# Two reorderings around the first triangular inverse: block reads behind the image reads, gate rows ahead of the crossed products

## The reference

```python
proj = h @ w_in                                   # q, k, v, z and two gates per head
qkv = silu(causal_dwconv(qkv, conv_w))            # 4 taps
q, k = l2_norm(q), l2_norm(k)                     # 8 key heads, 16 value heads of 128
g = -exp(a_log) * softplus(a + dt_bias);  beta = sigmoid(b)
g = cumsum(g);  decay = exp(g_i - g_j) below the diagonal
a = strict_lower((k_beta @ k.T) * decay)
t_inv = triangular_solve(eye + a, eye)            # inverse of a unit triangular matrix per head
u = t_inv @ v_beta;  w = t_inv @ (k_beta * exp(g))
# a scan over the chunks with a state per head, then
o = rms(o) * out_gain * silu(z);  out = o @ w_out
```

## Time and profile before

| | |
|---|---|
| time, median of 3 runs | 1376.77 us (1374.51 to 1379.86) |
| the profiled execution's own time | 1376.62 us |
| its span in the profile | 1374.7 us |
| PE busy / PEld busy | 97% / 83% of the span |
| DVE / ACT / POOL busy | 65% / 52% / 14% |
| mean granted TensorE clock | 0.991 |

### The profile page before, as it was taken

The page is one execution under the profiler, slowest core; times in us unless marked ns, Lnnn a source line. Parts: engine busy times, 40 slices in busy tenths (PEclk is TensorE's granted clock), DMA queues, the critical chain, the costliest instruction groups (busy, mean ns, idle before and its releaser), DMA issues.

```text
span 1374.7 us, 18871 instructions
## 1 busy us (share of the span) xinstructions
PE 1338.4 (97%) x7177; PEld 1134.7 (83%) x7177; DVE 894.2 (65%) x1539; ACT 710.1 (52%) x1209; POOL 190.4 (14%) x342
## 2 busy tenths in 40 slices
PE   9997989899999999999999999999999999999998
PEld 9897988778888888888888887888888877888887
DVE  7885888667555468475554699875554587755553
ACT  7764464326444346464444556654444466544441
POOL 2486888500200000000000000000000000000000
PEclk9998999999999999999999999999999999999999
DMA  9766655446665545255655455066555431566552
GB/s 267 190 157 154 150 156 148 116 131 186 186 187 189 181 140 188 87 182 185 188 185 185 151 184 170 23 214 187 182 190 187 166 123 62 165 202 184 186 191 83
DMA packets 172163, 226.46 MB, mean 165 GB/s; under 512 B 11832, under 2 KB 137594, under 8 KB 172074
## 3 DMA queue, kind: packets, MB, share of 16 engines
q1 hardware_dynamic: 166976, 213.03, 49.1%
q0 software_dynamic: 3328, 10.24, 3.7%
q10 hardware_dynamic: 1770, 1.99, 0.5%
HBM read 219.77 MB, written 5.45 MB: 164 GB/s over the span
## 4 chain that ended last, share of the span: by engine, by line
PE 76%; DVE 13%; POOL 3%; DMA 3%; issue 2%; ACT 2%; SPq 0%; ACTq 0%; DVEq 0%; POOLq 0%
PE psum L961 22%; PE psum L963 22%; PE psum L962 21%; DVE w_low L708 3%; PE psum L1194 2%; PE psum L1188 2%; POOL vectors L3285 1%; PE psum L1432 1%; PE psum L1392 1%; PE psum L1465 1%; DMA ring<-in_gdn_w_in 1%; POOL vectors L3282 1%; DVE arena L2740 1%; PE psum L952 1%; DVE work L880 1%
## 5 line engine op out<-in xcount | busy, mean ns | idle before, releaser
L708 DVE TENSOR_TENSOR w_low<-ring,w_high 128x1024 fp32r<-128x1024 f32 (+3 forms) x395 | 476.5, 1217 | 319.4 <-ACT w_high L694 319.1
L694 ACT ACTIVATE w_high<-ring 128x1024 fp32r<-128x1024 f32 (+3 forms) x395 | 410.7, 1048 | 421.0 <-PE psum L963 399.9
L961 PE MATMUL psum<-w_high,hT 128*128 128x512 f32 (+2 forms) x944 | 371.1, 393 | 0.0
L963 PE MATMUL psum<-w_high,hT 128*128 128x512 f32 (+2 forms) x944 | 366.0, 388 | 0.0
L962 PE MATMUL psum<-w_low,hT 128*128 128x512 f32 (+2 forms) x944 | 365.5, 387 | 0.0
L961 PE MATMUL psum<-w_high,parts 128*128 128x512 f32 (+1 forms) x532 | 210.3, 395 | 1.1 <-DVE parts L2748 1.1
L963 PEld LDWEIGHTS psum<-w_high,hT 128*128 128x128 f32 x944 | 177.2, 188 | 36.5
L963 PE MATMUL psum<-w_high,parts 128*128 128x512 f32 (+1 forms) x532 | 206.8, 389 | 0.0
L962 PE MATMUL psum<-w_low,parts 128*128 128x512 f32 (+1 forms) x532 | 206.7, 389 | 0.0
L962 PEld LDWEIGHTS psum<-w_low,hT 128*128 128x128 f32 x944 | 177.5, 188 | 33.8
L961 PEld LDWEIGHTS psum<-w_high,hT 128*128 128x128 f32 x944 | 177.4, 188 | 33.7
(11 more groups left out here) (306 smaller groups left out, 1402.4 us busy)
## 6 DMA issues: line engine op xcount, KB each, us to landing
ring<-in_ffn_w_gate_up SPq DMA_DIRECT2D x176, 256.0 KB, 3.2
ring<-in_w_gate_up SPq DMA_DIRECT2D x176, 256.0 KB, 3.2
ring<-in_gdn_w_in SPq DMA_DIRECT2D x48, 512.0 KB, 5.5
ring<-in_ffn_w_down SPq DMA_DIRECT2D x44, 512.0 KB, 3.2
ring<-in_w_down SPq DMA_DIRECT2D x44, 512.0 KB, 3.2
ring<-in_da_w_qkv SPq DMA_DIRECT2D x24, 512.0 KB, 3.7
ring<-in_gdn_w_out SPq DMA_DIRECT2D x16, 512.0 KB, 3.8
ring<-in_mla_w_out SPq DMA_DIRECT2D x8, 512.0 KB, 4.3
```

The costliest lines, as they stand in the source:

```text
L694: nc.scalar.activation(piece_slot(w_high, n), piece_slot(ring, n), ACT.Copy).then_inc(s.w_hi, 1)
L708: nc.vector.tensor_tensor(piece_slot(w_low, n), piece_slot(ring, n), piece_slot(w_high, n).bitcast(F32), ALU.subtract).then_inc(s.w_lo, 1)
L961: mm(out, lhs[0], rhs[0], start=start, stop=False)
L963: return mm(out, lhs[1], rhs[0], start=False, stop=stop)
```

## The change

Three lists are edited; no instruction is added, removed or changed in size.

- PE, `group_0`: `gate_rows(2)` now stands ahead of `crossed(0)` and no longer behind it.
- ACT: `gate_diff(2)` now stands between the tap of tile 19 and the split of the weight piece that follows it, so that it is ahead of the split.
- POOL: `blocks_in(1)` now stands behind `units_in()` and `images_in(0)`, and no longer ahead of them. DVE's and SP's lists are the same.

```diff
@@ PE, group_0 @@
                 turned_keys(2)
                 tile(19)
+                gate_rows(2)
                 crossed(0)
-                gate_rows(2)
                 tile(20, 0, 4)
@@ ACT @@
             z_pieces(1, 3)
-            tiles(19)
+            tap(19)
             gate_diff(2)
+            split_high(act, tile_piece[19] + SPLIT)
             gate_exp(2)
@@ POOL, loop over the groups @@
                 images_out(g)
-                if g == 0:
-                    blocks_in(1)
                 if g < GROUPS - 1:
                     units_in()
                 if g == 0:
                     images_in(0)
+                    blocks_in(1)
```

## The result

| | before | after |
|---|---|---|
| median of 20 runs each, us | 1374.96 | 1381.37 |
| lowest to highest, us | 1370.43 to 1381.31 | 1376.11 to 1388.48 |
| profiled execution: own time, span, us | 1376.62, 1374.7 | 1378.34, 1376.5 |
| its mean granted clock | 0.991 | 0.990 |

The ratio after to before is 1.0041, 95% interval 1.0027 to 1.0055: some 5.6 us slower. The forecast was no change. So neither stands for its kernel, and the experiments come back to that.

A forecast was written before the change was run, and what follows sets the result against it. PE, busy 97%, was taken as the bound. At group 1's first order, 0.5 of gain left, less 1.8 for the clock, plus 1.2 of small waits, gave -0.1: 1376.62 + 0.1 = 1376.7 us; range 1371.5 to 1381.5.

The forecast's parts named there:

- The steps at group 0: Group 0: x lands at 112, gate rows fill PE's gap, second order 8.8 us earlier, 10.3 gained at the recurrence.
- The late start: POOL, group 1: later block reads make the inversion start 3.5 us late, range 1 to 4.6, against 115.92.
- The collisions: POOL's stretch from group 1's inversion to its images: 11 slow overlaps with DVE against 8, three more costing 2.7 us.
- a slack of 6.7: Group 1: x lands at 172.1, crossed products began at 178.78, leaving 6.7 us before lateness of x matters.
- the 178.2: Slower rival, group 1: once x lands past 178.2, each further microsecond of POOL's lateness is PE's.
- The clock behind the gap: Group 1: after PE's wait of nearly 10 us, crossed products cost 3.78 instead of 2.02, losing 1.8 us.
- the small waits: PE, behind group 1's crossed products: waits of 0.68 on ACT and 0.48 on DVE vanish, giving 1.2 us back.
- From there nothing of POOL's is on the way: After group 3's keys, POOL 0.9 us late, at worst moving group 3's crossed products by 0.9, absorbed by DVE's wait.
- The 3.01 us on DVE: Group 3: PE's 3.01 us wait on DVE ahead of the first order takes up POOL's 0.9 us of lateness.
- The slower rival: POOL's lateness delays PE at group 1 and again at group 3, together about 5 us: 1381.5; chance 0.15.
- its two conditions: Slower rival: blocks landing at 120.5, 4.6 us late, and collisions costing 4.5 us, so x of group 1 lands at 181.2.
- The chance of 0.05 for slower by more than 0.5%: Whole kernel: slower than 1383.7 us, needing the slower rival and more; chance 0.05.

The follow-up runs named there:

- the second execution of before: The kernel before, nothing changed, profiled once more with one execution; measured 1375.62 us.
- the changed kernel's second profile: The kernel with all three edits, nothing further changed, profiled once more with one execution; measured 1378.14 us.
- PE held back: The full change plus 24 spare products on PE ahead of group 2's gate rows, some 6 us; 1383.11 us, ratio 1.0046.
- the rows alone: Only the PE and ACT edits against the kernel before, POOL's order as before; 1376.07 us, ratio 1.0000.
- POOL late: The kernel before plus 13 small POOL fills ahead of group 1's first copy, some 4.5 us; 1380.19 us, ratio 1.0022.
- the blocks in the inversion: The PE and ACT edits, with group 1's block reads issued at step 30 of group 0's inversion; 1373.41 us, ratio 0.9998 to before.
- the blocks by ACT: The PE and ACT edits, with group 1's two block reads issued by ACT on its own queue; 1371.80 us, ratio 0.9970 to before.
- blocks alone: Only the POOL edit against the kernel before, PE and ACT as before; 1382.29 us, ratio 1.0041.
- the kernels with the other queue: Block reads on ACT's queue with PE and ACT edits, 0.9970 to before; the same with group 3's half output product ahead of its crossed products, 0.9971.

## Why the prediction was wrong

The steps at group 0 were right. x was foreseen at 112, within 111.5 to 115.5, and by its row landed at 106.59 + 7.6 = 114.2, just as PE was ready (114.1). The reading took 7.6 us with no blocks ahead of it, so blocks ahead explain only 1.3 us of the 8.9, and the 4.9 of the next round was not to be had here. The rest was as foreseen: the gate rows in the gap, the crossed products at 113.9 and full clock (114.21, 2.05 us), the second order at 121.8 (122.43), a gain of 8.2 us there where 8.8 stood. PE came to the crossed products of group 1 at 166.17, even earlier than the 168.5 foreseen. Everything behind that came out worse.

**The late start, mis-sized.** POOL's copy was put at 119.4 and came at 120.42, at the very end of the range given: 4.5 us late for 3.5. The second read was issued at 110.53, inside the 109 to 111.5 foreseen, and took 9.8 us to land, where 119.4 leaves 8.9.

**The collisions, miscounted.** Three more were counted, 2.7 us; the stretch grew by 4.05. The price was about right. The count was read from a window of before that is shifted by PE's gain but has POOL's old length and end, 129.80 to 180.00. POOL's own lateness belongs into its end. A window to 183.8 has all 12 of the splits that lay beside POOL in the end:

```profile
129.70:183.80 54.10, 14.58 (x12) 0.97 0.58 139
```

Twelve against 7 is five more, and of the masking at 119.74 only the end still meets POOL's copy (0.61 us for 0.21). Five at 0.9, less the 0.5 of the masking, are 4.0. The Trainium skill ("SBUF — State Buffer", "Who interferes with whom") has a DVE operation with two inputs in SBUF contend with a GpSimd operation that reads SBUF, under an exclusive lock. The trace agrees: only POOL operations beside such DVE operations were long, as told above, and one that began at 169.99, 0.3 us into a split from 169.68 to 171.00, ended at 171.27. The 4.05 us for five, some 0.8 each, are less than the 1.22 of a split, as it would be if POOL comes some way into most of them.

Together x was issued 8.55 us late, not 6.2, against a slack of 6.7: it landed at 180.45 and not 178.3, past the 178.2 that the prediction names as the point from which each further microsecond is PE's. This is the step that put PE behind. Of the slack itself only 1.9 us are there in the second execution of before.

**The clock behind the gap, nearly right.** The crossed products cost 3.78, as foreseen. The gate rows behind them, priced at their old 2.02, took 2.80. How far the slow clock reaches varies: they took 2.43 in the changed kernel's second profile, behind the same gap, and 1.95 with PE held back, behind 12.34 us. The first order of group 1 was so 2.7 us late against the first execution, where the prediction's sum had it 0.1 us late: 1.7 for x, 1.8 and 0.8 for the clock, less 1.2 for the small waits and 0.4 of overlapped ends.

**"From there nothing of POOL's is on the way" failed too.** The prediction had POOL reach the keys of group 3 at 194.0 and DVE's matrices ready at 193.2. POOL came at 194.5, but the matrices were late: the writing started at 196.28 instead of 193.06. They hang on PE. In the eight profiles in which POOL waits there for DVE, the writing starts 7.6 to 8.4 us behind PE's first order of group 1, so PE's 2.7 us of lateness went by way of DVE back to POOL. X of group 3 was then issued 3.8 us late by the first profile of before, and 6.1 by the second (258.61 against 252.53). PE waited 2.54 us for it (3.19 in the second profile), and the crossed products took 3.52 us for 2.05; none of this stood in the sum. There was no room for it: x of group 3 landed at 259.4 in the first execution of before, and PE began on it at 259.42. In the second one PE, early, waits 3.40 us for it, as it waits 3.8 to 4.7 us with the rows alone, POOL late, the blocks in the inversion and the blocks by ACT. POOL late by hand, with hardly a gap of PE at group 1, cost some 3 us (0.1 to 5.8), which speaks for it too. The 3.01 us on DVE ahead of the first order did take up their share, against the first execution; in the second that wait isn't there.

**The base.** The sum was made against an execution whose first mixer took 4.7 us more than it did the second time. The lateness of the changed kernel against the two executions of before:

| PE at | against the first | against the second |
|---|---|---|
| first order of group 1 | 2.7 | 7.7 |
| first order of group 3 | 3.5 | 6.6 |
| L952 | 1.8 | 6.5 |

So the loss is made at group 1; group 3 only hands it on. The timed difference is 5.6. That the rows alone bring nothing has two reasons in their profile: at group 3 x is no earlier than in the second execution of before, so that PE's gain of 1 us at group 1 only lengthens that wait, and the tail is a slow one.

The forecast's mechanism was thus right up to x of group 1, with sizes that were too small, and wrong from there. The slower rival's was right: POOL's lateness past 178.2, later at group 3, with the crossed products cooled there (3.52 us at 264.65). It was priced at 1381.5 and the median is 1381.37, but it had a chance of 0.15. That the two agree so closely is luck, as its 5 us were added to 1376.62, and the median of before is 1374.96. The chance was too low because its two conditions, 4.6 us late and 4.5 of collisions, had been put at their far ends when the first was the edge of a range and the second came of a window read too short. The chance of 0.05 for slower by more than 0.5% was not tested by this result: the loss is within that bound.

## What to carry to other kernels

When a change makes one engine early and another late, follow the late one through all its later hand-overs to the last, and take as slack only what a second execution shows too (6.7 us here, then 1.9): an engine that does not wait may only have been slow by chance. When work is shifted past another engine's, the window in which collisions are counted must be moved at both ends, by the gain of the one and the lateness of the other. If two transfers want the same queue at the same time, give one another engine's queue before trying orders: each order here moved the wait to another place (full change, blocks alone, blocks in the inversion). Only the kernels with the other queue were faster than before, by 0.3%, and even they wait more for x at group 1 (6.79 and 8.35 us), because POOL, started earlier, met more splits.

## What the runs showed of the hardware

- A gap of PE does not always bring the slow clock. The crossed products took 2.05 us behind waits of 3.27 and 3.00 us, 2.87 behind 3.22, 3.58 behind 3.40, and 3.78 behind 4.70. With 2.54 us of wait they took 3.52. The gate rows right behind them took from 1.95 to 3.15 us behind gaps of 12.34 and 12.11.
- The same kernel varies by 11 us from run to run (1370.43 to 1381.31). The two profiles of before show short stretches with a granted clock of 0.5 to 0.9 where PE is busy and where the other execution had 1.00 (132 to 137, 1140 to 1170). Over all twelve profiles the latter window has a clock of 1.00, 0.89 or 0.72, and the tail behind L952 takes 1066, 1069 or 1072 us with it.
- POOL's two-input operations were more than 0.3 us longer (up to 1.1) only beside DVE operations of over 0.4 us with both inputs in SBUF, in 123 of 269 cases; the other 643 were never longer by more than 0.06 us.
- A block read of 220.5 KB took 9.8 us to land in POOL's queue behind the readings of x and y, 8.8 with neither ahead of it (before, issued at 107.10), 6.6 in ACT's queue, and 5.5 alone. The weights' queue had 61% of the DMA engines' time beside the second (107 to 120) and 10% beside the last (148 to 151.5), so what the queue and what the load adds isn't separated.
- The issue of the second block read sat 4.38 us in POOL's queue (3.34 in the second execution) and went out about 0.5 us after the writing of x had landed; behind the readings of x and y it did not sit at all. What held it isn't shown.
